# One step of a hybrid decoder on one core: the last expert's rows added by TensorE, the layer norm fused into the convolution, the last transfers halved

## The reference

```python
# layer 1's mixer
a = h @ w_pw1 + b_pw1
u = a[..., :1024] * sigmoid(a[..., 1024:])
c = depthwise_conv(concat(hist, u), w_dw, width=31) + b_dw
c = silu(layer_norm(c, ln_g, ln_b))          # over the 1024 channels
y = c @ w_pw2 + b_pw2
# mixture of experts, both layers
hid = silu(h @ w_gate[e]) * (h @ w_up[e])    # D_EXPERT = 256
out = out + combine[:, e:e+1] * (hid @ w_down[e])
```

## Time and profile before

| | us |
|---|---|
| median of 3 runs (lowest, highest) | 1061.65 (1059.97, 1063.12) |
| profiled execution, its own time | 1056.0 |
| its span, first to last instruction | 1054.2 |
| TensorE busy in the span | 910.0 (86%) |
| VectorE busy | 413.8 (39%) |
| ScalarE busy | 284.7 (27%) |
| POOL busy | 274.2 (26%) |
| mean granted TensorE clock | 0.942 of full |

### The profile page before, as it was taken

The page is one execution under the profiler, slowest core; times in us unless marked ns, Lnnn a source line. Parts: engine busy times, 40 slices in busy tenths (PEclk is TensorE's granted clock), DMA queues, the critical chain, the costliest instruction groups (busy, mean ns, idle before and its releaser), DMA issues. The chain is left out here.

```text
span 1054.2 us, 18744 instructions
## 1 busy us (share of the span) xinstructions
PE 910.0 (86%) x7258; PEld 664.7 (63%) x7258; DVE 413.8 (39%) x951; ACT 284.7 (27%) x591; POOL 274.2 (26%) x424
## 2 busy tenths in 40 slices
PE   7999999966998888884899999679869988897885
PEld 6988888954555555552787878269645555554553
DVE  5266784274111111112768786753551111111114
ACT  6355672131121111111521111352411111111103
POOL 1810000014432343211234343220133432342110
PEclk9999999997998999998689999989969999999998
DMA  7522112686999999995734452426859999999956
GB/s 235 179 44 51 42 42 73 248 353 249 412 415 417 418 412 415 420 421 191 217 84 125 121 132 73 96 63 241 358 205 388 414 416 418 417 416 419 420 224 254
DMA packets 111700, 277.70 MB, mean 263 GB/s; under 512 B 34888, under 2 KB 73112, under 8 KB 86986
## 3 DMA queue, kind: packets, MB, share of 16 engines
q1 hardware_dynamic: 96054, 253.74, 63.1%
q0 software_dynamic: 11424, 17.87, 4.7%
q10 hardware_dynamic: 4132, 4.86, 1.9%
HBM read 266.25 MB, written 27.45 MB: 279 GB/s over the span
## 5 line engine op out<-in xcount | busy, mean ns | idle before, releaser
L1988 DVE COPY areaB<-ps 128x512 f32<-128x512 f32 x66 | 45.6, 692 | 359.4 <-PE ps L1971 359.4
L1954 PE MATMUL ps<-ring,areaB 128*64 128x256 f32 x640 | 153.7, 396 | 26.7 <-issue 24.5
L1955 PE MATMUL ps<-ring,areaB 128*64 128x256 f32 x640 | 154.2, 397 | 0.0
L2000 POOL DMA_INDIRECT pair_rows<-areaB,idx x66 | 67.6, 1024 | 266.7 <-DVE areaB L1988 256.7
L1954 PEld LDWEIGHTS ps<-ring,areaB 128*64 128x64 f32 x640 | 87.8, 142 | 69.1 <-issue 29.3
L1979 ACT ACTIVATE v_rows<-ps 128x256 f32<-128x256 f32 x66 | 25.3, 383 | 274.5 <-PE ps L1955 274.5
L1055 PE MATMUL ps<-conv_x_high,pw_halves 128*128 128x272 f32 x512 | 89.7, 296 | 1.6 <-DVE areaS L1259 1.6
L1955 PEld LDWEIGHTS ps<-ring,areaB 128*64 128x64 f32 x640 | 87.9, 142 | 0.0
L1995 POOL DMA_INDIRECT areaC<-h_rows,idx x66 | 68.7, 1040 | 56.1 <-issue 45.7
L1976 ACT ACTIVATE areaB<-ps 128x512 f32<-128x512 f32 x66 | 39.4, 597 | 149.0 <-PE ps L1946 149.0
L1971 PE MATMUL ps<-ring,areaB 128*64 128x512 f32 x320 | 76.1, 593 | 1.6 <-DVE areaB L1985 1.6
(11 more groups left out here) (360 smaller groups left out, 1814.4 us busy)
## 6 DMA issues: line engine op xcount, KB each, us to landing
ring<-in_w_gate SPq DMA_DIRECT2D x40, 1024.0 KB, 25.3
ring<-in_w_up SPq DMA_DIRECT2D x40, 1024.0 KB, 28.0
ring<-in_w_down SPq DMA_DIRECT2D x40, 1024.0 KB, 26.9
areaA<-in_w_gate SPq DMA_DIRECT2D x12, 1024.0 KB, 21.0
areaA<-in_w_up SPq DMA_DIRECT2D x12, 1024.0 KB, 25.3
wring<-in_w_down SPq DMA_DIRECT2D x12, 1024.0 KB, 21.9
h_T<-in_w_gate SPq DMA_DIRECT2D x12, 1024.0 KB, 22.9
h_T<-in_w_up SPq DMA_DIRECT2D x12, 1024.0 KB, 25.2
```

What stands on the lines that cost most here:

```text
L1954: pe.matmul(ps[0:CAP, 2 + odd, 0:F], rows, ring_gate(ws)[:, k, :], start=(k == 0), stop=(k == KT - 1))
L1955: mm = pe.matmul(ps[CAP:P, 2 + odd, 0:F], rows, ring_up(ws)[:, k, :], start=(k == 0), stop=(k == KT - 1))
L1988: return v.tensor_copy(rows_out[:, s, :], ps[:, 5 + odd, :])
L2000: return gp.indirect_dma_start(pair_half_rows, bass.IndirectOffsetOnAxis(idx[:, RING + s:RING + 1 + s], 0), rows_out[:, s, :], None, bound ...
```

## The change

- **Last expert's rows.** The last tile (32) is no longer scattered. `weigh_late` (VectorE, in tile 10's step) builds a token-by-slot matrix of the weights of the pairs that this expert's first 64 rows serve, and takes those weights out of `weight`; TensorE turns it in tiles 12 and 14, ScalarE copies it to `late_T` (slots by tokens, twice, in partitions 0 to 63 and 64 to 127). At the end TensorE multiplies the last tile's rows with it: in layer 0 eight `late(j)` groups, whose results VectorE adds to `x_T`; in layer 1 two matmuls a token tile into the banks that hold x. `pair_rows` is filled once with x in the attention stage, so that rows never scattered hold numbers.
- **Pair rows loaded ahead.** SP loads them when tile 31's down is done and all scatters but the last have landed.
- **Order.** In the last tile's step tile 31's down projection, and in layer 1 two of the x turns, go ahead of gate and up.
- **Halved transfers.** The last expert's gate and up come in two halves of k, and TensorE waits for each half.
- **Fused layer norm.** `layernorm_project_stage` becomes a helper of the convolution stage, with no barrier between. The channels are shifted by a mean over the first four tiles (`EARLY`); POOL adds the shift (`shift_away`), ScalarE squares, POOL sums the squares of tiles 0 to 6 (`gather_squares`) while the convolution runs. The last tile is squared by itself, and the variance is corrected by the distance of the means. Tiles are centred inside the scaling loop. `keep_warm` is three matmuls whose result nobody reads.
- Semaphores of these stages are cleared by POOL in the routing stage.

```diff
@@ attention stage, SP
                     for i in range(6, NW):
                         sp.wait_ge(w_ready[i % 2], i // 2)
                         load_weights(sp, i)
+                        if i < 10:
+                            c, a = (i - 6) // 2, (i - 6) % 2
+                            sp.dma_start(pair_rows[c * T + a * NP // 2:c * T + (a + 1) * NP // 2, :],
+                                         x_prompt2[a * NP // 2:(a + 1) * NP // 2, :]).then_inc(pairs_filled, 16)
+                            if a:
+                                sp.dma_start(pair_rows[c * T + NP:(c + 1) * T, :], x_sample2).then_inc(pairs_filled, 16)
@@ convolution stage, SP, TensorE and ScalarE
+                        if k == KT - 1:
+                            for i in range(2):
+                                sp.wait_ge(cols.ready[i], KT)
+                            first_columns(sp, "w_pw2", w_pw2[0], (0, P), columns_landed["w_pw2"])
                         load_quads(sp, k, (0, 1))
...
+                        if k == EARLY:
+                            pe.wait_ge(shift_ready, 1)
+                            pe.wait_ge(squares_gathered, 1)
+                            for c in range(2):
+                                pe.matmul(sum_banks[:, c, :], shift_back, shift[0:1, c * TH:(c + 1) * TH], start=True, stop=False)
...
+                        if k == EARLY + 1:
+                            act.wait_ge(summed, 2)
+                            nc.scalar.activation(half(shift), sum_banks, ACT.Copy, scale=-1.0 / (EARLY * P)).then_inc(shift_ready, 1)
+                        if k == EARLY + 2:
+                            for j in range(EARLY + 1):
+                                square_away(j)
@@ convolution stage, VectorE and POOL
                         if k == KT - 1:
+                            v.wait_ge(u_done, 2 * KT)
+                            ln.keep_fresh(v)
+                            ln.cols.low(v, 0, 0)
                             finish(k - 1)
...
+                        if k == EARLY + 1:
+                            for j in range(EARLY):
+                                shift_away(j)
+                        if k == EARLY + 2:
+                            shift_away(EARLY)
+                            gather_squares(0, 1)
+                            gather_squares(2, 3)
+                            gather_squares(0, 2)
+                            shift_away(EARLY + 1)
+                            gather_squares(0, EARLY)
+                    shift_away(KT - 2)
+                    for j in range(EARLY + 1, KT - 1):
+                        gather_squares(0, j)
@@ layer norm, TensorE
+                    def keep_warm():
+                        for _ in range(3):
+                            pe.matmul(ps[:, 3, :], ident[:, :], x_T[:, 0, 0:512], start=True, stop=True)
+
+                    pe.wait_ge(u_kept, 2)
+                    pe.wait_ge(squares_gathered, self.GATHERED)
+                    square_sums(away[:, 0, :], True)
+                    last_sums().then_inc(ln_summed, 1)
+                    pe.wait_ge(ln_squared, 1)
+                    square_sums(far_last, False).then_inc(ln_summed, 1)
+                    keep_warm()
                     pe.wait_ge(inverted, 1)
...
                     mm.then_inc(spread, 1)
+                    keep_warm()
@@ layer norm, VectorE
+                    v.wait_ge(squares_gathered, 4)
+                    step.done(v.tensor_tensor(far_last, c_T[:, KT - 1, :], shift, ALU.add))
+                    cols.low(v, 1, 0)
+                    v.wait_ge(ln_summed, 1)
+                    for c in range(2):
+                        at = slice(64 * c, 64 * c + 64)
+                        step.done(v.scalar_tensor_tensor(far_mean[at], mean_sums[at, c, :], 1.0 / D, shift[at, c * TH:(c + 1) * TH],
+                                                         ALU.mult, ALU.add))
+                    step.wait()
+                    step.link(v.tensor_tensor(far_mean, far_mean, far_mean, ALU.mult))
+                    v.wait_ge(ln_summed, 2)
+                    step.link(v.scalar_tensor_tensor(rstd_rows, squares, 1.0 / D, far_mean, ALU.mult, ALU.subtract))
+                    step.done(v.tensor_scalar(rstd_rows, rstd_rows, 0.0, None, ALU.max))
+                    centre(0)
                     v.wait_ge(rooted, 1)
                     v.reciprocal(rstd_rows, rstd_rows).then_inc(inverted, 1)
+                    centre(1)
                     v.wait_ge(spread, 1)
                     for k in range(KT + 2):
                         if k < KT:
+                            if k > 1:
+                                centre(k)
@@ to_stream, TensorE
+                    def late(j):
+                        k = LATE_KS[j]
+                        at = slice(k // 4 * CAP, (k // 4 + 1) * CAP)
+                        after(pe, late_added, j - 1)
+                        for c in range(2):
+                            mm = pe.matmul(late_banks(j)[:, c, :], late_rows[at, (k % 4) * P:(k % 4 + 1) * P], late_T[at, c * TH:(c + 1) * TH],
+                                           start=True, stop=True)
+                        mm.then_inc(late_made, 1)
+
+                    pe.wait_ge(late_kept, 2)
+                    pe.wait_ge(out_kept, NCH)
+                    turn(0)
+                    for j in range(4):
+                        late(j)
+                    turn(1)
+                    for j in range(4, KT):
+                        late(j)
+                    for i in range(2, NT):
+                        turn(i)
@@ to_outputs, TensorE
+                def before_last(self, pe):
+                    self.turn_x(pe, 1)
+                    pe.wait_ge(out_kept, NCH - 1)
+                    self.turn_x(pe, 0)
...
+                        if i >= 2:
+                            self.turn_x(pe, i)
+                        for c in range(2):
+                            at = slice(c * CAP, (c + 1) * CAP)
+                            pe.matmul(banks(i)[0:r, c, :], late_T[at, t * P:t * P + r], late_rows[at, :], start=False, stop=False)
@@ expert stage, SP and TensorE
+                            for a in range(2):
+                                ks = slice(a * KT // 2, (a + 1) * KT // 2)
+                                for dst, w in ((ring_gate, w_gate), (ring_up, w_up)):
+                                    src = w[l, ds(expert, 1)].rearrange("e (p k) f -> p (e k) f", p=P)[:, ks, :]
+                                    sp.dma_start(dst(position % RING)[:, ks, :], src).then_inc(last_half_landed[a], 16)
...
+                    sp.wait_ge(down_done, last)
+                    sp.wait_ge(early_rows_stored, 1)
+                    load_pairs(sp, l)
                     more.sync(sp, spill_of(sp))
-                    sp.wait_ge(rows_complete, 1)
-                    load_pairs(sp, l)
...
+                        if final:
+                            out(x.shift(-1))
+                            combine.before_last(pe)
                         pe.wait_ge(turned_kept, x.e + 1)
```

More of the change, by code:

```diff
@@ L1092, in conv_stage @@
             sum_banks = ps[:, 6:8, 0:TH]
+            EARLY = 4
+            away = h_T
+            shift, shift_back = h_T[:, KT - 1, :], areaS[0:1, 1888:1888 + P]
+            ln = layernorm_project_stage(1, cols, squares_gathered, away, shift)
             col = lambda k, n: chan[:, k, n:n + 1]
@@ L1389, in _, with tensor, square_sums @@
                     mm.then_inc(u_turned, 1)
-                    for k in range(KT):
-                        pe.wait_ge(ln_squared, k + 1)
+                def tensor(self, pe, last_sums):
+                    def square_sums(row, first):
                         for c in range(2):
-                            mm = pe.matmul(ps[64 * c:64 * c + 64, 4, 0:TH], ones[:, 0:64], ln_sq[:, k % 2, c * TH:(c + 1) * TH],
-                                           start=(k == 0), stop=(k == KT - 1))
-                        mm.then_inc(ln_summed, 1)
+                            mm = pe.matmul(squares[64 * c:64 * c + 64, :], ones[:, 0:64], row[:, c * TH:(c + 1) * TH], start=first, stop=not first)
+                        return mm
+                    def keep_warm():
[8 more added lines that the diff above has]
+                    keep_warm()
                     pe.wait_ge(inverted, 1)
@@ L1500, in _ @@
                     square(3, False, True)
+            return Project()
         area_route = areaS[:, :]
@@ L1816, in mix @@
                         v.wait_ge(first_scaled, i + 1)
[L1817 to L1818 removed]
+                        v.scalar_tensor_tensor(pair(t)[0:r, 0, :], pair(t)[0:r, 1, :], weight[0:r, NT + t:NT + t + 1],
+                                               pair(t)[0:r, 0, :], ALU.mult, ALU.add).then_inc(mixed, 1)
                     def add(i):
@@ L2243, in body @@
                             sp.dma_start(dst, rows_by_partition(src, l, e)).then_inc(o["landed"], 16)
-                    self.over(sp, spilled, body)
```

(1 more changed line is left out.)

329 lines of the change are left out of this document (217 added, 112 removed).

## The result

The changed kernel takes 1056.1 us against 1061.4 (medians of 20 runs each). The ratio of the two is put at 0.9955, 95% interval 0.9936 to 0.9975, that is -4.8 us (-6.8 to -2.7); the two medians alone lie 5.3 apart. Forecast were -11.9. So 1056.1 lies inside the wide range with the rivals (1043.5 to 1057.5) and outside the forecast's own (1046 to 1054). The profiled execution took 1053.4 us, span 1051.6.

The account below looks back on a forecast made before the run. Weight DMA was taken to bound the expert stages, so only the layers' ends and layer norm could gain: -10.0-2.0-0.3+0.4 = -11.9, giving 1049.7 us. Own range 1046 to 1054; with rivals 1043.5 to 1057.5.

Parts of the forecast that it names:

- I take -2.0: End of layer 0: tile 31's earlier down projection and pair loads, with late groups replacing the scatter, gain 2.0 us.
- rival 1: End of layer 0: TensorE's clock falls and stays at 1.2 GHz, last add 516.5, kernel 1056; chance 0.13.
- 1.8 us of TensorE's idle time that stays: End of layer 0: turn(0) waits for the first mix and holds late groups that could start at 487.3.
- In a gap of 8 us: Convolution's end: `first_columns` for pw2 moves ahead of tile 7's quads on SP, in an 8 us gap, costing nothing.
- the layer norm: Between convolution and projection: fusion shortens the chain by 8.1 us, the held clock gives 2.3, POOL lateness costs 0.4: -10.0.
- Rival 2: Convolution: POOL contends with VectorE in all 13 operations, 7.8 us late less 1 of cover, kernel 1056.5; chance 0.10.
- the end of layer 1: Last rows out 3.2 us later, then late pairs, weighting pairs and x turns on TensorE; net +0.4 us.
- rival 3: End of layer 1: the row halves of late pairs don't overlap on TensorE, +4.4 us, kernel 1054.1; chance 0.07.
- at nothing: Work counted as hidden at no cost, such as six x copies in attention; halved transfers also counted 0.
- Rival 4: Attention: x copies on the SP queue hold the query weights, +16 us at 14 us a copy, kernel 1066; chance 0.05.
- the -0.3 of the convolution's first product: Start of the convolution, after layer 0's end: its first product gains another 0.3 us.

Follow-up runs that it names:

- `fused_only`: The kernel before with the fused layer norm alone, both ends of the layers as before; ratio to the kernel before 0.9936 (0.9912 to 0.9960).
- `shift_back_late`: The changed kernel with the four shift matmuls moved from tile 4's sums to behind tile 6's; ratio to the kernel before 0.9946 (0.9922 to 0.9971).

## Why the prediction was wrong

- **The failed step: "I take -2.0"** for the end of layer 0. Its stretch cost +2.5. The three sums that I had made differ by the clock alone: 509.2 at 2.4 GHz, 511.2 with recovery, 516.5 at 1.2 GHz for the last add's end; measured 515.21. I held the low clock for unlikely because of one row, a wait of 2.60 us before an expert behind which TensorE kept its speed; I even wrote that 2.7 us were less than that, which they are not. The clock fell all the same, in all eight profiles of this order, behind waits of 2.8 to 3.3 us. And the row was one execution: in the three other profiles of that code the clock fell at this very expert, behind 2.30 and 3.29 us. This was rival 1, given 0.13, with 1056. That the median is 1056.1 is in part luck: the end of layer 0 missed by 4.5 us and not by 6.5, and the convolution, which no rival had, gave 2.7 more.
- **A sum that does not come out:** the terms written for 2.4 GHz (three mixes and four adds behind the last late addition) end at 509.9, not at 509.2. This moves neither the forecast nor the reading of it by as much as 1 us.
- **The order of the groups** stood in the forecast only as "1.8 us of TensorE's idle time that stays". The new order took 7.5 us (27.9 to 20.4) out of the tail, 5.9 in the profile with the lowest clock; that is more than holding the clock gave in that order (1.9 to 3.5), and about as much or more than I estimate for it in the old one (4 to 5). I had summed TensorE's groups and VectorE's mixes one behind the other as the code has them, and not asked what the sum would be if the mixes lay in VectorE's waits for the groups.
- **Left out: the matmuls that put the shift back.** Four in 1.18 us in a round where TensorE is never idle: +1.1. I had costed VectorE's, ScalarE's and POOL's new work in the convolution and not TensorE's.
- **Left out: the wait before the last taps**, +1.6 in the mean: the quads 0.3 to 2.4 us late, and the taps at a lower clock in some executions (6.2 us in place of 4.5). "In a gap of 8 us" was said of the weights moved ahead of the quads; `fused_only` has them too, with taps at 9.43, so alone they are not the cause. Which of the two parts' additions delays the issue when they meet stays open.
- **Right: the layer norm**, -10.0 forecast and measured, with its parts: 7.3 us to the scaling (7.4), 2.5 for the clock (2.3), POOL not late in the changed kernel: by the contention its last sample step ends 1.1 us later behind tile 7's value (1.2 forecast), and its chain ends at 675.9, ahead of VectorE's last sum at 679.2. Rival 2 (POOL contends in all its operations) did not come, but its mechanism showed as soon as `shift_back_late` moved the round.
- **Right: the end of layer 1**, +0.1 for +0.4: the last rows +3.0 (3.2), the rest -2.9 (-2.8), row halves overlap (rival 3 out).
- **Right: at nothing** for halved transfers and the x copies: the first turn of expert rows comes 0.3 us later (246.4 for 246.1 in the mean of 16 and 4 profiles). Rival 4 is out.
- **Not resolved:** the -0.3 of the convolution's first product. In the two profiles of the changed kernel it runs at 2.4 GHz nearly from its start (granted clock 1.00 and 0.94 in its first 6 us, 0.80 in both of the kernel before). The stretch to tile 6's value is 0.4 us shorter in the mean (128.2 to 127.8), in a scatter of 2.0.
- **Not forecast: the gain ahead of the last rows** in layer 0, -2.2. I had counted some 1.1 us for the down projection that moved. That it also fills a wait behind which the clock fell in three of four old profiles I could not see in the one trace that I had.

## What to carry to other kernels

Where two engines hand work to and fro, cost the order as its own term: lay out both engines' work side by side, and put what needs neither (here the mixes) into the waits. That was worth at least as much as the clock here, and both together made the kernel 1.3% faster than before in place of 0.45%. Do not rest a forecast on one wait behind which the clock held in one execution: the same wait lost it in others. Added work on the engine that is never idle is paid in full however short it is, and work moved off it may meet another engine's port. To place a few us, compare stretches between two events over several profiles, not spans.

## What the runs showed of the hardware

- The length of the one wait ahead did not tell whether TensorE's granted clock falls to 1.2 GHz. It fell behind waits of 2.8 to 3.3 us in the tail (all eight profiles), and at the last gate and up behind 2.30, 3.29 and 3.29 us but not behind 2.60. The last taps ran at 2.4 GHz (4.50 us) behind waits of 0.3 to 3.6 us in 15 profiles and took 5.85 to 6.20 in five, with waits of 2.0 to 3.0 us.
- A VectorE instruction with two SBUF operands, 0.75 us alone, took 1.73 beside a POOL addition of 1.35 that had started 0.17 us ahead of it.
- Issuing eight transfers of 66 KB took 5.3 us in six profiles and up to 7.0 us in others with the same instructions; this stays open.
